# Transposing, squaring and normalising the tokens of the first layer tile by tile, with the last tile inside the value projection

## What is computed

```python
def rmsnorm(x, w):
    y = x * lax.rsqrt(jnp.mean(x * x, axis=-1, keepdims=True) + EPS)
    return y * w
# each layer, D_MODEL = 1024:
h = rmsnorm(x, norm_mix_w)
z, xbc, dt_raw, q, k, v = split_in(h @ w_in)
x = x + [ssd_branch(z, xbc, dt_raw) | rmsnorm(attention(q, k, v))] @ w_out
x = x + ffn(rmsnorm(x, norm_ffn_w))      # dense SwiGLU, then top-2-of-8 experts
```

## Time and profile before

| what | us |
|---|---|
| median of the timed runs | 1563.59 |
| the profiled execution | 1576.77 |
| its span, first to last instruction | 1575.1 |
| PE busy | 1538.7 (98% of the span) |
| first PE work begins | 9.67 |
| value projection begins, L732 | 20.37 |
| key projection begins, L717 | 27.84 |

### The profile page before, as it was taken

How to read it: one execution, slowest core, us unless ns; L and a number is a source line. 1 busy time by engine, 2 the same in 40 slices (tenths; PEclk the granted TensorE clock), 3 DMA queues, 4 the chain that set the end, 5 groups by cost and what they waited for, 6 DMA issues and landing times.

```text
span 1575.1 us, 44436 instructions
## 1 busy us (share of the span) xinstructions
PE 1538.7 (98%) x20568; PEld 1297.8 (82%) x20568; DVE 282.2 (18%) x680; ACT 206.0 (13%) x530; POOL 131.0 (8%) x200
## 2 busy tenths in 40 slices
PE   7999999999999999999999999999999999999998
PEld 5677666666666666767999999999999999999897
DVE  2454620000000245564000000000000000000021
ACT  1245310000000024533000000000000000000000
POOL 4211125000000020112000000000000000000100
PEclk9999999999999999999999999999999999999999
DMA  9933429976333422343999999999999999999991
GB/s 263 254 112 100 127 88 276 333 254 222 108 107 107 121 89 92 90 130 116 333 362 349 362 360 347 370 347 350 352 348 357 354 353 361 349 366 355 345 347 36
DMA packets 199227, 397.39 MB, mean 252 GB/s; under 512 B 13722, under 2 KB 69666, under 8 KB 198888
## 3 DMA queue, kind: packets, MB, share of 16 engines
q1 hardware_dynamic: 180664, 346.26, 64.3%
q0 software_dynamic: 16816, 45.42, 9.6%
q10 hardware_dynamic: 1568, 2.91, 0.6%
HBM read 359.87 MB, written 36.63 MB: 252 GB/s over the span
## 4 chain that ended last, share of the span: by engine, by line
PE 95%; DVE 2%; issue 1%; ACT 1%; DMA 0%; SPq 0%; ACTq 0%; DVEq 0%
PE bank L1299 34%; PE bank L1321 17%; PE bank L1212 13%; PE bank L763 7%; PE bank L1229 6%; PE bank L746 2%; PE bank L1076 2%; PE bank L1059 2%; PE bank L732 1%; PE bank L1031 1%; PE bank L1043 1%; PE bank L717 1%; PE bank L686 1%; PE bank L1335 0%; PE bank L1049 0%
## 5 line engine op out<-in xcount | busy, mean ns | idle before, releaser
L1299 PE MATMUL bank<-arena,ring 128*64 128x108 f32 x11264 | 533.6, 258 | 10.3 <-issue 9.4
L1299 PEld LDWEIGHTS bank<-arena,ring 128*64 128x64 f32 x11264 | 527.2, 138 | 16.4 <-issue 14.7
L1321 PE MATMUL bank<-arena,ring 128*64 128x108 f32 x5632 | 262.7, 256 | 0.0
L1321 PEld LDWEIGHTS bank<-arena,ring 128*64 128x64 f32 x5632 | 261.4, 137 | 0.3
L1212 PE MATMUL bank<-hnT,ring 128*128 128x336 f32 x704 | 199.1, 446 | 1.8 <-DVE hnT L1683 1.8
L1212 PEld LDWEIGHTS bank<-hnT,ring 128*128 128x128 f32 x704 | 133.8, 190 | 67.2 <-issue 2.3
L763 PE MATMUL bank<-hnT,ring 128*128 128x336 f32 x384 | 119.8, 457 | 0.0
L2138 DVE TENSOR_TENSOR arena<-arena,bank 128x432 f32<-128x432 f32 (+1 forms) x48 | 27.2, 567 | 506.1 <-PE bank L1299 506.1
L1229 PE MATMUL bank<-arena,ring 128*128 128x336 f32 x352 | 99.6, 446 | 0.0
L763 PEld LDWEIGHTS bank<-hnT,ring 128*128 128x128 f32 x384 | 70.6, 192 | 34.6 <-issue 6.3
L1229 PEld LDWEIGHTS bank<-arena,ring 128*128 128x128 f32 x352 | 66.9, 190 | 32.5
(11 more groups left out here) (360 smaller groups left out, 1063.8 us busy)
## 6 DMA issues: line engine op xcount, KB each, us to landing
ring<-in_moe_w_gate SPq DMA_DIRECT2D x88, 1024.0 KB, 6.3
ring<-in_moe_w_up SPq DMA_DIRECT2D x88, 1024.0 KB, 6.4
ring<-in_moe_w_down SPq DMA_DIRECT2D x88, 1024.0 KB, 5.9
ring<-in_w_in SPq DMA_DIRECT2D x16, 1024.0 KB, 7.2
ring<-in_w_gate SPq DMA_DIRECT2D x11, 1024.0 KB, 21.0
ring<-in_w_up SPq DMA_DIRECT2D x11, 1024.0 KB, 18.7
xg_rows<-arena POOLq DMA_DIRECT2D x1, 10800.0 KB, 71.2
y_rows<-arena POOLq DMA_DIRECT2D x1, 10800.0 KB, 113.2
```

Of the source, the lines that this page charges most:

```text
L1299: ins = mm(into[rows, SLOTS * fi:SLOTS * fi + SLOTS], weights[:, c, col:col + 64], xg[:, k0 + c, :], start=(k0 + c == 0 and fi == 0), stop ...
L1321: ins = mm(bank[5 + c // 4][rows, SLOTS * (c % 4):SLOTS * (c % 4) + SLOTS], weights[:, col:col + 64], hid[:, f, :], start=(f == 0 and c % ...
```

## The change

The tokens get three semaphores, one for each tile. PE transposes tile 0 and tile 1 as their rows come (8 transposes each, four chunks of features to a bank), then sums the squares of tile 0 and tile 1 (8 matmuls of 128 columns each), then the parameters; the convolution rows and the transposes of tile 2 follow. In the value projection, PE does tile 0, then the sums of tile 2 (8 matmuls of 80 columns), then tile 1, then tile 2. The wait for the copied convolution rows (`prev_ready`) now stands ahead of the key projection. DVE copies a tile in two instructions (512 columns, or 320 for tile 2), makes `hnT` for the first 256 tokens in 8 instructions, copies tile 2, and then makes its `hnT` in 8 more. ACT squares half a tile at a time and makes `rstd` in two parts. The seven parameter loads of layer 1 move from ACT's queue to SP's, behind the loads of slabs 0 and 1. POOL waits for two transposed halves in place of four chunks. Layer 1 keeps its order; only counts are moved.

```diff
             for n, loads in enumerate(fixed):
+                if n == 2:
+                    with nc.allow_non_contiguous_dma(reason="small tables"):
+                        param_rows(sp, 1)
                 if n == 4:
                     sp.dma_start(const[:, 128:], a["const"][:, 128:]).then_inc(const_here, 16)
...
-                pool.wait_ge(xin_psum, 4)
+                pool.wait_ge(xin_psum, 2)
...
-            pe.wait_ge(tokens_here, 80)
-            for k in range(DK):
-                if k >= 4:
-                    pe.wait_ge(xT_ready, k - 3)
-                for i, (t0, n) in enumerate(TILES):
-                    ins = nc.tensor.transpose(bank[1 + k % 4][:, t0:t0 + n], xtok_in[0:n, i, 128 * k:128 * k + 128], ident[0:n, 0:n])
-                ins.then_inc(xin_psum, 1)
+            def tokens_turned(i):
+                n = TILES[i][1]
+                pe.wait_ge(tokens_here[i], (32, 16, 32)[i])
+                for k in range(DK):
+                    ins = nc.tensor.transpose(turned_tokens(i, k // 4)[:, k % 4, :], xtok_in[0:n, i, 128 * k:128 * k + 128], ident[0:n, 0:n])
+                    if k % 4 == 3:
+                        ins.then_inc(xin_psum, 1)
+            def token_sums(i):
+                t0, n = TILES[i]
+                for k in range(DK):
+                    if k % 4 == 0:
+                        pe.wait_ge(squares_ready, tokens_done(i, k // 4))
+                    ins = mm(bank[0][:, t0:t0 + n], ones[:, :], squares[0][:, k, t0:t0 + n], start=(k == 0), stop=(k == DK - 1))
+                return ins
+            tokens_turned(0)
+            tokens_turned(1)
+            token_sums(0)
+            token_sums(1).then_inc(sum_psum, 1)
             pe.wait_ge(params_here, 16 * 7 * LAYERS)
...
-                pe.wait_ge(prev_ready, l + 1)
+                if l:
+                    pe.wait_ge(prev_ready, l + 1)
+                else:
+                    tokens_turned(2)
...
                         if i == 0:
-                            pe.wait_ge(hn_ready, 8 * 2 * l + k + 1)
+                            pe.wait_ge(hn_ready, 24 * l + k + 1)
+                        elif i == 2 and l == 0:
+                            pe.wait_ge(hn_ready, 8 + k + 1)
                         ins = mm(bank[1][0:n, 136 * i:136 * i + 136], hnT[:, k, t0:t0 + n], vdt[:, k, :], start=(k == 0), stop=(k == DK - 1))
+                    if i == 0 and l == 0:
+                        token_sums(2).then_inc(sum_psum, 1)
                 ins.then_inc(proj_psum, 1)
+                if l == 0:
+                    pe.wait_ge(prev_ready, 1)
...
+                def tokens_squared(i):
+                    t0, n = TILES[i]
+                    for half in range(2):
+                        act.wait_ge(xT_ready, tokens_done(i, half))
+                        f(squares[0][:, 4 * half:4 * half + 4, t0:t0 + n], xT[:, 4 * half:4 * half + 4, t0:t0 + n], ACT.Square).then_inc(squares_ready, 1 + i // 2)
+                tokens_squared(0)
+                tokens_squared(1)
+                for part, cols in enumerate((slice(0, 256), slice(256, NT))):
+                    if part:
+                        tokens_squared(2)
+                    act.wait_ge(sum_psum, part + 1)
+                    link(f(out[:, cols], bank[0][:, cols], ACT.Ln, scale=1.0 / D, bias=eps))
+                    f(out[:, cols], out[:, cols], ACT.Exp, scale=-0.5).then_inc(rstd_ready, 1)
...
+            def tokens_kept(i):
+                t0, n = TILES[i]
+                for half in range(2):
+                    dve.wait_ge(xin_psum, 2 * i + half + 1)
+                    v.tensor_copy(xT[:, 4 * half:4 * half + 4, t0:t0 + n], turned_tokens(i, half)).then_inc(xT_ready, 1 + i // 2)
+            tokens_kept(0)
+            tokens_kept(1)
...
+                    normed(0, R_MIX, rstd, 1, slice(0, 256))
+                    tokens_kept(2)
+                    dve.wait_ge(xT_ready, 8)
+                    normed(0, R_MIX, rstd, 2, slice(256, NT))
                 link(v.memset(raw[:, :, 0:3], 0.0))
                 dve.wait_ge(prev_psum, l + 1)
```

More of the change, by code:

```diff
@@ L378, in hymba_step @@
         slab_free = sem("slab_free")
-        ident_here, const_here, tokens_here, params_here, small_here, sinks_here = (
-            sem(x) for x in ("ident_here", "const_here", "tokens_here", "params_here", "small_here", "sinks_here"))
+        ident_here, const_here, params_here, small_here, sinks_here = (
+            sem(x) for x in ("ident_here", "const_here", "params_here", "small_here", "sinks_here"))
+        tokens_here = [sem(f"tokens_here{i}") for i in range(3)]
         conv_rows_here, caches_here, router_here = sem("conv_rows_here"), [sem(f"caches_here{i}") for i in range(2)], sem("router_here")
@@ L421, in hymba_step, with turned_tokens, prev_rows, tokens_done @@
         dve_step, act_step = sem("dve_step"), sem("act_step")
+        def turned_tokens(i, half):
+            n = TILES[i][1]
+            return bank[1 + 2 * i + half][:, 0:4 * n].rearrange("p (k t) -> p k t", k=4)
+        def prev_rows(l):
+            return bank[1 if l else 2][:, 0:192]
+        def tokens_done(i, half):
+            return (1, 2, 3, 4, 6, 8)[2 * i + half]
         def sstate_bank(pr, q):
@@ L434, in wait_slab, with param_rows, row @@
             pe.wait_ge(slab_here[n % RING], arrives[n])
+        def param_rows(engine, l):
+            prow = conv_[:, 128:256]
+            r = PARAM_ROWS * l
+            def row(r0, n, src):
+                engine.dma_start(prow[r + r0:r + r0 + n, :], src).then_inc(params_here, 16)
+            row(R_MIX, 8, a["norm_mix_w"][l].rearrange("(k p) -> k p", p=128))
+            row(R_FFN, 8, a["norm_ffn_w"][l].rearrange("(k p) -> k p", p=128))
+            row(R_CW, 32, a["conv_w"][l].rearrange("w (k p) -> (w k) p", p=128))
+            row(R_CB, 8, a["conv_b"][l].rearrange("(k p) -> k p", p=128))
+            row(R_SSD, 4, a["ssd_norm_w"][l].rearrange("(k p) -> k p", p=128))
+            for g in range(2):
+                engine.dma_start(prow[r + R_ATT:r + R_ATT + 4, 64 * g:64 * g + 64],
+                                 a["attn_norm_w"][l][256 * g:256 * g + 256].rearrange("(c d) -> c d", d=64)).then_inc(params_here, 16)
         @block.sync
@@ L1247, in _ @@
             ins.then_inc(count_psum, 1)
-            pe.wait_ge(rstd_ready, 4)
+            pe.wait_ge(rstd_ready, 5)
             for i, (t0, n) in enumerate(TILES):
@@ L1377, in _ @@
                 act.dma_start(ident, a["const"][:, 0:128]).then_inc(ident_here, 16)
[L1378 to L1392, removed]
+                param_rows(act, 0)
             def half_rows(i, half):
@@ L1415, in _ @@
                     act.wait_ge(rows_blank, 32)
-                norm(2 * l, rstd)
+                    norm(2 * l, rstd)
+                else:
+                    first_norm(rstd)
                 def decay_rows_wanted(pr):
@@ L1671, in _, with normed @@
             dve.wait_ge(set_up, 3)
-            for k in range(DK):
-                dve.wait_ge(xin_psum, k + 1)
-                v.tensor_copy(xT[:, k, :], bank[1 + k % 4][:, 0:NT]).then_inc(xT_ready, 1)
+            def tokens_kept(i):
[5 more added lines that the diff above has]
+            tokens_kept(1)
             dve.wait_ge(params_psum, 1)
             link(v.tensor_copy(params[:, :], bank[7][:, 0:128]))
-            def normed(n, l, r0, scale):
-                dve.wait_ge(rstd_ready, n + 1)
+            def normed(l, r0, scale, roots, cols=slice(0, NT)):
+                dve.wait_ge(rstd_ready, roots)
                 for k in range(DK):
                     c = PARAM_ROWS * l + r0 + k
-                    v.scalar_tensor_tensor(out=hnT[:, k, :], in0=xT[:, k, :], scalar=params[:, c:c + 1], in1=scale,
+                    v.scalar_tensor_tensor(out=hnT[:, k, cols], in0=xT[:, k, cols], scalar=params[:, c:c + 1], in1=scale[:, cols],
                                            op0=ALU.mult, op1=ALU.mult).then_inc(hn_ready, 1)
@@ L1695, in _ @@
                 for r in range(3):
-                    ins = v.tensor_copy(raw[:, :, S0 + r:S0 + r + 78:11], bank[1][:, 0:192].rearrange("p (k b r) -> p k b r", k=DK, r=3)[:, :, :, r])
+                    ins = v.tensor_copy(raw[:, :, S0 + r:S0 + r + 78:11], prev_rows(l).rearrange("p (k b r) -> p k b r", k=DK, r=3)[:, :, :, r])
                     (ins.then_inc(prev_ready, 1) if r == 2 else None)
-                normed(2 * l, l, R_MIX, rstd)
+                if l:
+                    normed(l, R_MIX, rstd, 4)
                 dve.wait_ge(small_here, 16 * 9 * (l + 1))
@@ L2032, in _ @@
                 if l == 0:
-                    normed(2 * l + 1, l, R_FFN, rstd_f)
+                    normed(l, R_FFN, rstd_f, 3)
                     for i in range(2):
```

29 lines of the change are left out of this document (17 added, 12 removed).

## The result

The changed kernel took 1573.55 us (median of 5 runs, 1569.30 to 1575.28) against 1563.59 us (5 runs, 1562.60 to 1567.98). The ratio is 1.0047, 95% interval 1.0027 to 1.0066, so it is slower by 4 to 10 us where 2 us less was forecast. In a later comparison, beside its variants, it came out at 1.0022 (1.0007 to 1.0037), slower by 1 to 6 us.

A forecast was written before the change was run, and what follows sets the result against it. PE was taken as the bound, 95% of the chain. `hnT` start 16.0 plus 9.85 puts the key projection at 25.85 instead of 27.84, 2.0 us earlier, giving 1561.5 us, range 1557.5 to 1566.0.

The forecast's parts named there:

- What bounds the kernel: Whole run: PE is 95% of the chain; its work from the key projection on stays the same, so that projection's start decides.
- Transposes and sums: PE's opening: tile 1's transposes 7.9 to 9.5, sums of tiles 0 and 1 from 9.5 to 15.0, range 14.25 to 16.0.
- rival 4: Token loads: tile 0's rows land no sooner than the last, the change does nothing, 1565.2 us; chance 0.03.
- `rstd`: ACT, first 256 tokens: Ln 0.47 and Exp 0.42; with hand-overs, `hnT` starts 1.0 us after the sums, at 16.0.
- The parameters: Layer 1's seven loads on SP: issued by about 12.4, landed at 14.4 (13.9 to 16.2), ready at 15.15, hidden by the sums.
- what carries the gain on: After the opening: slab 3 keeps 5 us of cover; POOL's tables issued some 5 us earlier, DVE's wait shrinks at no gain.
- From `normed` to the key projection: PE's value projection with tile 2's sums inside: the key projection starts 9.85 us after `hnT` starts, before 8.2.
- H + 9.85: Start of the key projection on PE, H being the start of `hnT`, forecast at 16.0; together 25.85.
- rival 1: PE's clock: late rise (sums to 16.0) and a fall to half clock in the value projection, 1563.9, no gain; chance 0.14.
- Rival 2: SP held in the seven small issues: landing near 23.6, key projection at 34.2, 6.3 us later, 1569.9; chance 0.07.
- The cover of slab 3: Weight load for L746: lands by 27.4 at the latest, wanted from 32.5 on, so 5 us of cover remain.

## Why the prediction was wrong, point by point

- **What bounds the kernel: right, but the shift is not carried whole.** PE's opening is on the path. At the first matmul of layer 0's dense feed-forward (L1212 before, L1269 after) the two profiles of the changed kernel are 3.4 and 3.3 us behind those of before (226.42 for 223.02, 226.93 for 223.67), where the openings differ by 5.0 and 4.9. In between, each profile of before has one short piece at half clock, and those of the changed kernel have none. In the first profile of before it is this one, where 8 entries took 1.97 us that took 1.12 in the changed kernel:

```profile
153.19:156.60 3.41, 3.41 (x17) 3.41 (x18) 3.41 (x8) 1.80 (x6) 0.00 (x0) 0.50 0.33 107
```

  The text held PE's later work to be the same before and after, and so left out that pieces at half clock come and go. Behind this point come the experts with their scatter.
- **Transposes and sums: 1 us too early.** Tile 0's transposes began at 5.38, so its rows landed sooner on their own semaphore, and rival 4 falls. Tile 1's transposes began at 8.57, not 7.9, and between 8.2 and 9.8 in all variants. The sums began at 10.33, not 9.5, and ended at 16.03 where 15.0 was forecast and 16.0 was the late end. The clock rose near 14.4, where 13.0 was taken: PE did 12 entries in the 2 us from 12 to 14, and 10 in the 1 us from 15 to 16. In the seven variants of the changed kernel the rise came between 11.8 and 13.2, so the spread that the text allowed (11.5 to 15) was right.
- **`rstd`: right.** 0.97 us after the sums, forecast 1.0.
- **The parameters: the step that failed.** The text bounded the landing by 13.9 and 16.2 (its own terms, 12.0 and 4.1, give 16.1), from the landings of slab 1 and of the tokens, took 14.4, and held it to be hidden by the sums; it was 20.6, and PE stood still for 4.59 us. SP issued them as foretold (done at 12.92, forecast 12.4). What was left out stands in the text's own paragraph on what carries the gain on, where POOL's tables "are issued some 5 us earlier ... at no gain": it was weighed as a wait of DVE and not as traffic. Of the 7.0 us between the forecast opening of 25.85 and 32.89, 4.3 are `normed` waiting past 17.0, 1.0 the later sums, and 1.7 the stretch from `normed` on, of which the next point tells.
- **From `normed` to the key projection: right but for the clock.** H + 9.85 was forecast; with the parameters on ACT, at full clock, it was 10.04 (26.20 - 16.16). In the changed kernel it was 11.57 (32.89 - 21.32), at half clock from 21.3 to 28.1, and 11.04 in its second profile (33.40 - 22.36): rival 1's mechanism, but behind the wait for the parameters. In the variants of the changed kernel without that wait this stretch ran at full clock.
- **Rival 2 had the right point and the wrong reason.** It said that the change turns slower once the parameters land later than 17.2, and so it came. But it held SP's issue to be the cause; SP's seven issues took 0.3 us each but for the first (1.62), and what was slow was the landing. Its chance, 0.07, was that of the wrong mechanism, and that its numbers (landing near 23.6, opening 34.2) lie near the measured 20.6 and 32.89 is luck.
- **The cover of slab 3 was enough.** No wait of PE for slabs 2 and 3 appears in any profile's opening.

**What stays open.** The three variants with the parameters on SP and no long wait for them have openings of 26.40, 26.43 and 26.01, about as good as those with the parameters on ACT, yet ratios of 0.9996, 1.0004 and 1.0005, where the four with the parameters on ACT have 0.9979 to 0.9988. The difference, some 3 us, is about what the intervals allow. It may be that the landing on SP's queue is late in some executions that were not profiled, or that the weights behind it come later (theory D). The profiles show no sign of the second ahead of the experts: the first expert's matmuls begin at 740.64 with all tables late and at 740.16 with the spread rows late, against 740.47 with the parameters on ACT. (In the other variants this point lies between 738.22 and 745.06, so it scatters too.) No run settles it. Nor is it settled why the first comparison gave 7 us by its ratio (10 by the medians) and the second 3.4 (3.8), beyond that both intervals hold the 5.0 of the opening.

## What to carry to other kernels

When a wait is relaxed, ask not only who waited but what the waiting engine will issue, and what else is in flight then: here a GpSimd wait moved from four transposed chunks to two halves sent nine tiny loads, five of them slow, into the path of seven others. Keep a load that gates the whole pipeline away from loads that spread one row over partitions, however small it is. Standing behind a slab on its queue cost much less here: an opening of 26.43 in place of 25.76. And for an effect of a few microseconds in a run with stalls elsewhere, compare the same stretch of several profiles, not their spans.

## What the runs showed of the hardware

- A tiny load can hold the DMA engines far out of proportion to its bytes: 192 packets with 0.01 MB took 74.4% of 16 engines for 7.5 us, and all queues together moved 0.09 MB at 12 GB/s, where the same stretch without them carried 257 GB/s. It was the loads that spread a row: 80 packets of 64 or 256 bytes with 1.2 us each in the mean, 69 of them begun in that stretch. 59 packets in the same stretch without these took 0.9%.
- PE's standstill was paid twice here. After 4.59 and 5.79 us without work, the clock was at 0.50 for 6.8 us in both profiles of the changed kernel, which cost their openings another 1.5 and 1.0 us (11.57 and 11.04 from `normed` to the key projection in place of 10.04).
- Short pieces at half clock come at other places in another profile of the same kernel: between the opening and 220 us, the first profile of before has 3.4 us at 0.50 from 153.2, the second from 68.7, and the two of the changed kernel none. By then some 1.6 of their 5.0 us were gone.
- Two profiles of one kernel differed by 9 us in span with openings equal to 0.6 us.
